# Constant products in five waits of the tensor engine: a two-block transformer kernel on one core

## The reference, cut to what matters

```python
def second_block(x, c, ctx, ...):
    h = x
    for layer in range(2):
        sh1, sc1, g1, sh2, sc2, g2 = ada_mod(c, ada_w[layer], ada_b[layer])
        xn = modulate(rms_norm_2(h, norm_mix_g[layer]), sh1, sc1)
        if layer % 2 == 0:
            y, _ = even_mixer(xn, xcn, mix_in_w, mix_out_w, ...)   # Fourier mix and window attention
        else:
            y = pool_mix(xn, pool_w, pool_scale)                   # windowed means, then 4 products
        h = h + g1 * y
        hn = modulate(rms_norm_2(h, norm_ffn_g[layer]), sh2, sc2)
        h = h + g2 * swiglu(hn, ffn_w1[layer], ffn_w3[layer], ffn_w2[layer])
    return rms_norm_2(h, final_g)

def swiglu(h, w1, w3, w2):
    return (jax.nn.silu(h @ w1) * (h @ w3)) @ w2
```

## Time and profile before

| what | value |
|---|---|
| device time, median of 3 runs | 1762.76 us (1761.27 to 1765.35) |
| the profiled execution | 1751.8 us, its span 1750.0 us |
| mean granted PE clock over the span | 0.891 |
| PE busy | 1381.0 us (79%), 10631 matmuls |
| DVE busy | 628.7 us (36%) |
| ACT busy | 164.3 us (9%) |
| moved by DMA | 590.07 MB, mean 337 GB/s |
| chain that ended last | DMA 48%, PE 44%, DVE 5%, ACT 2%, issue 1% |

### The profile page before, as it was taken

One profiled execution on the slowest core, in us unless ns is written; L12 is line 12 of the kernel. 1 busy time (PEld: TensorE's weight loads), 2 busy tenths in 40 slices (PEclk: granted clock), 3 DMA queues, 4 the chain that ended last, 5 costly groups with the idle time before them and its releaser, 6 DMA issues.

```text
span 1750.0 us, 24372 instructions
## 1 busy us (share of the span) xinstructions
PE 1381.0 (79%) x10631; PEld 861.6 (49%) x10631; DVE 628.7 (36%) x984; ACT 164.3 (9%) x413; POOL 5.0 (0%) x10
## 2 busy tenths in 40 slices
PE   6798998766676666766666567668998999889997
PEld 4787853322122212221222122216876999879997
DVE  2367642601010101010101010107446877768775
ACT  2003321100000000000000000002521000120001
POOL 1000000000000000000000000000000000000000
PEclk8998998888688868887888788889999999999999
DMA  9989957999999999999999999997944555414541
GB/s 401 365 335 402 407 230 298 396 431 431 431 431 431 431 431 431 431 431 431 431 431 431 431 431 431 431 430 282 404 164 151 206 207 188 172 70 164 210 176 63
DMA packets 46554, 590.07 MB, mean 337 GB/s; under 512 B 5360, under 2 KB 7824, under 8 KB 9376
## 3 DMA queue, kind: packets, MB, share of 16 engines
q1 hardware_dynamic: 42896, 583.89, 80.3%
q10 hardware_dynamic: 3600, 5.34, 0.9%
HBM read 586.58 MB, written 2.62 MB: 337 GB/s over the span
## 4 chain that ended last, share of the span: by engine, by line
DMA 48%; PE 44%; DVE 5%; ACT 2%; issue 1%; SPq 0%; DVEq 0%; ACTq 0%
DMA ring<-in_w 45%; PE ps L1985 5%; PE ps L1980 5%; PE ps L1981 5%; PE ps L1516 3%; PE ps L1689 3%; PE ps L1784 3%; PE ps L1804 3%; PE ps L1458 3%; PE ps L1996 2%; PE ps L1999 2%; PE ps L1998 2%; DMA ring<-in_w_in 2%; DMA ring<-in_w_ada 1%; DVE ring_parts L810 1%
## 5 line engine op out<-in xcount | busy, mean ns | idle before, releaser
L1784 PE MATMUL ps<-ring,mixT 128*32 128x512 f32 x2016 | 297.6, 726 | 166.6 <-DMA ring<-in_w 164.3
L1804 PE MATMUL ps<-ring,arena 128*32 128x512 f32 x1024 | 173.6, 815 | 106.3 <-DMA ring<-in_w 95.2
L1784 PEld LDWEIGHTS ps<-ring,mixT 128*32 128x32 f32 x2016 | 61.1, 121 | 377.1 <-DMA ring<-in_w 252.7
L810 DVE TENSOR_TENSOR ring_parts<-ring,ring_parts 128x1024 fp32r<-128x1024 f32 (+3 forms) x119 | 189.6, 1625 | 1.1
L1178 DVE TENSOR_TENSOR arena<-arena,ps 128x512 f32<-128x512 f32 x16 | 11.0, 687 | 495.8 <-PE ps L1784 495.8
L1980 PE MATMUL ps<-mixT_parts,ring_parts 128*128 128x256 f32 x704 | 171.0, 282 | 6.7 <-issue 6.7
L1981 PE MATMUL ps<-mixT_parts,ring_parts 128*128 128x256 f32 x704 | 170.8, 282 | 0.0
L1804 PEld LDWEIGHTS ps<-ring,arena 128*32 128x32 f32 x1024 | 33.0, 130 | 228.5 <-DMA ring<-in_w 146.5
L807 DVE CAST ring_parts<-ring 128x1024 fp32r<-128x1024 f32 (+3 forms) x119 | 100.3, 890 | 113.6 <-DMA ring<-in_f 72.2
L1980 PEld LDWEIGHTS ps<-mixT_parts,ring_parts 128*128 128x128 f32 x704 | 134.4, 191 | 7.9 <-issue 7.1
L1981 PEld LDWEIGHTS ps<-mixT_parts,ring_parts 128*128 128x128 f32 x704 | 134.0, 190 | 0.8
(11 more groups left out here) (359 smaller groups left out, 1374.0 us busy)
## 6 DMA issues: line engine op xcount, KB each, us to landing
ring<-in_w SPq DMA_DIRECT2D x190, 2048.0 KB, 25.7
ring<-in_ada_w SPq DMA_DIRECT2D x24, 2048.0 KB, 12.1
ring<-in_f SPq DMA_DIRECT2D x22, 2048.0 KB, 7.7
ring<-in_w_ada SPq DMA_DIRECT2D x12, 2048.0 KB, 16.5
ring<-in_f SPq DMA_DIRECT2D x22, 1024.0 KB, 5.5
ring<-in_w_in SPq DMA_DIRECT2D x5, 2048.0 KB, 22.9
ring<-in_w_out SPq DMA_DIRECT2D x2, 2048.0 KB, 11.4
ring<-in_mix_in SPq DMA_DIRECT2D x2, 2048.0 KB, 22.0
```

The lines of the kernel that those rows point to most:

```text
L810: return tt(out.bitcast(F32R), v, hi, ALU.subtract)
L1784: last = mm(ps[rows[u], j, :], XeT[:, 2 * m + k, rows[u]], w[:, u, k * FE:(k + 1) * FE], start=(m == 0 and k == 0), stop=(m == 3 and k == 1))
L1804: last = mm(ps[rows[u], m, :], heT[:, k, rows[u]], w[:, u, m * 512:(m + 1) * 512], start=(k == 0), stop=(k == FE // P - 1))
```

## The change

A new helper `busy(bank, n)` issues n float32 products of 256 columns, with two constants of the table `con` as operands (the identity and a slice of `sel`) and a PSUM bank as output. It counts no semaphore and nobody reads what it writes; the next real use of the bank begins with `start=True`, which overwrites it. Nothing else is changed, on any engine; the one added wait, for `nrm_xn` 9, stands ahead of the one for 10 that was there.

```diff
+            def busy(bank, n):
+
+                for _ in range(n):
+                    mm(ps[:, bank, 0:256], ident, C("sel")[:, 0:256], start=True, stop=True)
+
...
+            busy(1, 8)
             pe.wait_ge(h_split, 1)
             features(RW[1], 512, 2, 2, low_parts(1, 1))
...
             pe.wait_ge(g_ev, 3)
             gate_row(1, 10, 2)
+            busy(0, 3)
             norm_tr(3, 4)
+            busy(0, 7)
             pe.wait_ge(g_ev, 4)
             ffn(0)
             gate_row(2, 4, 2)
+            busy(0, 6)
+            pe.wait_ge(nrm_xn, 9)
+            busy(0, 2)
             pe.wait_ge(nrm_xn, 10)
             pe.wait_ge(pool_in, 32)
...
             last.then_inc(p_tr, 1)
+            busy(0, 4)
             pe.wait_ge(p_T, 2)
             pe.wait_ge(g_ev, 5)
...
                 last.then_inc(p_y, 1)
+            busy(4, 5)
             pe.wait_ge(x_new, 5 * NT)
             gate_row(2, 10, 2)
             norm_tr(5, 4)
+            busy(0, 7)
             pe.wait_ge(g_ev, 6)
             ffn(1)
```

## The result

| | median | runs |
|---|---|---|
| before | 1761.27 us (1754.93 to 1765.57) | 13 |
| changed | 1749.69 us (1744.51 to 1756.12) | 13 |

Single runs of one kernel lie up to 16 us apart (1751.5 to 1767.8 in the 143 runs of the kernel before), so the profiled run of before (1751.8 us) was an early one of its kind and that of the changed kernel (1755.85 us) a late one. The two traces compare stage by stage, not as a whole.

The account below looks back on a forecast made before the run. DMA was taken to bound 300 to 1183 us, PE the feed-forwards, with hand-to-hand waits between stages. Gains of 1.94 + 1.72 + 1.7 = 5.4 us, subtracted from 1762.76, gave 1757.4 us; range 1754.0 to 1761.3.

Parts of the forecast that it names:

- The step that failed: Whole kernel: the change can remove only time PE works at granted clock 0.50 behind waits; all gains summed to 5.4 us.
- The front's clock term: First projection, from 45.50 us: clock expected down again, DVE's low weights set the pace; gain 0, bounds 0 and 1.5 us.
- The second block: ffn(0), the pooling, and layer two's gate row and transposes: 1.94 + 1.72 + 1.7 = 5.4 us gained.
- pooling and gate row: Second block: 3.90 us at clock 0.56 in each, restored to full clock; 1.72 us and 1.7 us gained.
- `ffn(0)`: Its start, first product to second group: 5.25 us would become 3.31 at full clock, as in `ffn(1)`; gain 1.94 us.
- the start of `ffn(1)`: Second feed-forward, behind norm_tr(5): already at the full clock in the profile of before, so gain 0.
- Rival 2: Second block: one of three clock falls absent before, or `ffn(0)` waits for DVE; less gain, 1759.3 us, chance 0.16.
- Rivals 3 and 4: PE's waits: transposes don't hold the clock, 1763.1, chance 0.07; clock falls despite products, groups run at half, 1769.4, chance 0.05.
- The range: Whole kernel's median: 1754.0 to 1761.3 us, 1.8 us either side for run spread; cases left out had 0.18.

Follow-up runs that it names:

- run 143: Not a numbered run but a count: the kernel before, unchanged, was run 143 times; single runs lie between 1751.5 and 1767.8 us.

## Why the prediction was wrong

- **The step that failed** is the sentence that the change "can take away only what is lost behind a wait: the time in which PE works at a granted clock of 0.50". The added products are also instructions, and those ahead of the first projection moved the place behind the experts' loop at which PE stands still. That term was missing: 3.8 us (1.8 either way), measured by products that do almost no work. With the 7.3 us that the seven other groups gave in the timed runs it makes 11.1, against 10.8 for the whole change (its mean against that of the 143 runs). The rows for it were in the trace of before: 1.77 us of idle time put down to "issue" between two transposes that need no semaphore. I had no row of it in the list and explained "issue" only where a semaphore was the reason.
- **The front's clock term** was 0, with bounds of 0 and 1.5. That held: with the full clock all through, and with none of it, the means are 0.6 us apart (2.0 either way). The reason fits the rows: DVE and the transfers set the pace. In the profile of the changed kernel the first burst behind the products ran at the full clock (1.16 us), but the second took 2.01, at the half, where the working had both at the full; at 45.5 the clock was down, as expected.
- **The second block.** The sum was 5.4 us. In the profiles of the five kernels with all seven groups the last part takes 421.5, 422.4, 422.8, 420.8 and 421.3 us, in the nine without any 426.2 to 429.4: means 421.8 and 427.9, a gain of 6.2 us. The timed runs of the seven alone are 7.3 us below the mean of before, with 2.5 either way. By place: pooling and gate row 1.7 + 1.7, from the gate row behind `ffn(0)` to `ffn(1)` 35.46 us before and 32.15 after, 3.3. In the profiles without these groups this stretch takes 35.4 to 36.8, so it is 4.1 in the mean. `ffn(0)` was 1.94 by its own start; the stage from its first product to the gate row behind it gained 186.37 - 185.20 = 1.2, and 1.1 in the mean of the profiles. PE waits 0.2 us for DVE once more in there; where the other half microsecond went I didn't find. From the start of `ffn(1)` to the end the means are 196.0 and 195.1, 0.9 us for a term put at 0.
- **Rival 2**, that only part repeats, went the other way: other runs lost more. The start of `ffn(1)` was at the full clock in the profiled run and so put at 0. But in seven of the nine profiles without these groups its first 3 us read 0.50 to 0.53; the profile of before was one of the two exceptions. In the profiles the groups next to `norm_tr` give 1.1 + 0.9 = 2.0 us for the two feed-forwards, in the timed runs 3.9 with 1.7 either way; whether that last difference is more than noise stays open.
- **Rivals 3 and 4** did not occur. Transposes hold or don't hold the clock by themselves, the runs don't say; with products around them it stayed at 1.00 in each of the places. None of the seven groups ran at half clock.
- **The range** covered a spread of 2 us around the median for one forecast and its rivals, all of them about the clock. (By its own terms it would be 1754.1 to 1761.1 instead of 1754.0 to 1761.3; that changes nothing.) It had no room for a second mechanism.

## What to carry to other kernels

Here products of constants in waits of known length kept the clock, and cost nothing where they ended before the wait did: 6 us in the profiles, for 34 products. And four instructions without any work, added far ahead of a loop, were worth as much as eight full products there, since they moved a stop behind the loop. Before a gain is put down to what the instructions do, time them once with almost no work in them and once behind the place in question. And one profile is one draw: take the length of a stage from several before you call a place free of a loss.

## What was not expected of the hardware

- Behind the experts' loop, with the DMA engines at a share of 0.96 to 1.01, PE stood still for 1.74 to 5.51 us in seven of the eight profiles with nothing added ahead, after one transpose of eight. Four more instructions ahead of it, in a program of 10631 matmuls, took this stop away and made the kernel 0.22% faster (0.05 to 0.39). That it is the fetch of a block of code is the reading that fits the packets (PE goes on 1.2 to 1.5 us behind the end of one), the place and the shifts; the fetch itself was not varied.
- The kernel before, run 143 times, lies between 1751.5 and 1767.8 us. Taking the stop away doesn't narrow this for certain: 36 runs of the three kernels with full products in front lie between 1750.4 and 1762.0 us, but the 24 with small ones between 1749.1 and 1763.4, and as wide around their mean (standard deviation 4.1 against 3.7) as the kernel before.
- The clock at the start of `ffn(0)` was at 0.50 to 0.53 in all nine profiles without the seven groups, behind a wait of 3.3 us (1.9 where small products stand in it), and at the start of `ffn(1)` in seven of them, behind a wait of the same length.
